# Centring a group norm ahead of a linear recurrence, by a matrix in the turning of the values

## What is computed

```python
def wkv_scan(s0, r, w, k, v, a, b, reverse):
    def step(s, inp):
        r_t, w_t, k_t, v_t, a_t, b_t = inp
        sa = jnp.einsum('bhvk,bhk->bhv', s, a_t)
        s = s * w_t[:, :, None, :] + sa[..., :, None] * b_t[:, :, None, :] + v_t[..., :, None] * k_t[:, :, None, :]
        return s, jnp.einsum('bhvk,bhk->bhv', s, r_t)
...
def rwkv_out(y, r, k_sum, v, xg, g_up, r_k, gn_g, gn_b):
    mu = jnp.mean(y, axis=-1, keepdims=True)
    var = jnp.mean(jnp.square(y - mu), axis=-1, keepdims=True)
    yn = ((y - mu) * lax.rsqrt(var + GN_EPS)).reshape(bsz, t, D_RWKV) * gn_g + gn_b
    bonus = (jnp.sum(r * k_sum * r_k, axis=-1, keepdims=True) * v).reshape(bsz, t, D_RWKV)
    return (yn + bonus) * g
```

## Time and profile before

| what | us |
|---|---|
| three runs | 2332.89, 2322.07, 2326.87 |
| median | 2326.87 |
| span of the profiled execution, first to last instruction | 2324.3 |
| TensorE busy | 2102.2 (90%) |
| VectorE busy | 1575.8 (68%) |
| ScalarE busy | 1245.2 (54%) |
| 40 turnings (L582), each | 0.272 |
| 16 records of the mean products (L1377), together | 7.11 |

### The profile page before, as it was taken

How to read it: one execution, slowest core, us unless ns; L and a number is a source line. 1 busy time by engine, 2 the same in 40 slices (tenths; PEclk the granted TensorE clock), 3 DMA queues, 4 the chain that set the end, 5 groups by cost and what they waited for, 6 DMA issues and landing times. The chain is left out here.

```text
span 2324.3 us, 51473 instructions
## 1 busy us (share of the span) xinstructions
PE 2102.2 (90%) x21654; PEld 1675.4 (72%) x21654; DVE 1575.8 (68%) x2324; ACT 1245.2 (54%) x2324; POOL 659.5 (28%) x465
## 2 busy tenths in 40 slices
PE   5999999599999988891799999999958999999989
PEld 3788888477888853681688888888747778866667
DVE  3666654788889746427599999999766846556531
ACT  4422221476677654433688888888645434357530
POOL 0000020566666610114013323323034455400011
PEclk8999999799999999996899999999979999999999
DMA  8222252333222239426599999999845364230032
GB/s 287 59 68 61 71 130 47 74 72 72 64 64 65 58 110 354 146 100 235 208 354 384 389 397 388 387 395 392 280 132 179 105 221 115 88 131 2 2 110 81
DMA packets 164658, 399.63 MB, mean 172 GB/s; under 512 B 13630, under 2 KB 58060, under 8 KB 164428
## 3 DMA queue, kind: packets, MB, share of 16 engines
q1 hardware_dynamic: 149804, 347.56, 43.0%
q0 software_dynamic: 12224, 44.57, 7.0%
q10 hardware_dynamic: 2400, 4.21, 0.5%
HBM read 348.06 MB, written 46.66 MB: 170 GB/s over the span
## 5 line engine op out<-in xcount | busy, mean ns | idle before, releaser
L1940 DVE TENSOR_TENSOR exp_w_lo<-mixT,exp_w_hi 128x2048 fp32r<-128x2048 f32 x124 | 278.7, 2283 | 23.4 <-ACT exp_w_hi L1897 23.4
L1897 ACT ACTIVATE exp_w_hi<-mixT 128x1024 fp32r<-128x1024 f32 x256 | 255.0, 1053 | 55.8 <-PE banks L1859 38.6
L2153 POOL TENSOR_TENSOR w_lo<-mixT,w_hi 128x512 fp32r<-128x512 f32 (+1 forms) x108 | 145.7, 1370 | 166.6 <-ACT w_hi L2229 163.9
L1859 PE MATMUL banks<-exp_w_hi,xsT_lo 128*128 128x512 f32 x512 | 161.0, 396 | 6.3 <-DVE xsT_lo L1944 6.3
L1859 PE MATMUL banks<-exp_w_lo,xsT_hi 128*128 128x512 f32 x512 | 159.4, 393 | 0.0
L1859 PE MATMUL banks<-exp_w_hi,xsT_hi 128*128 128x512 f32 x512 | 159.3, 393 | 0.0
L1827 POOL DMA_INDIRECT moe_rows<-exp_out,idxT x16 | 25.2, 1573 | 435.7 <-DVE exp_out L1999 435.7
L2211 PE MATMUL banks<-w_hi,h_lo 128*128 128x512 f32 (+1 forms) x320 | 123.5, 386 | 7.8 <-POOL w_lo L2153 5.3
L2211 PE MATMUL banks<-w_lo,h_hi 128*128 128x512 f32 (+1 forms) x320 | 120.3, 376 | 0.0
L2211 PE MATMUL banks<-w_hi,h_hi 128*128 128x512 f32 (+1 forms) x320 | 120.2, 376 | 0.0
L1812 POOL DMA_INDIRECT xs<-xn_rows,idxT x16 | 116.0, 7248 | 14.2 <-DVE idxT L1971 5.6
(11 more groups left out here) (395 smaller groups left out, 5857.7 us busy)
## 6 DMA issues: line engine op xcount, KB each, us to landing
mixT<-in_exp_w_up_dram SPq DMA_DIRECT2D x62, 1024.0 KB, 10.2
mixT<-in_exp_w_gate_dram SPq DMA_DIRECT2D x34, 1024.0 KB, 9.3
mixT<-in_exp_w_down_dram SPq DMA_DIRECT2D x32, 1024.0 KB, 9.2
mixT<-in_w_in_dram SPq DMA_DIRECT2D x96, 256.0 KB, 2.9
ada_w_second<-in_ada_w_dram SPq DMA_DIRECT2D x16, 1024.0 KB, 9.6
kaT<-in_exp_w_down_dram SPq DMA_DIRECT2D x16, 1024.0 KB, 7.1
exp_w<-in_exp_w_down_dram SPq DMA_DIRECT2D x16, 1024.0 KB, 7.4
chunk<-rkv_scratch SPq DMA_DIRECT2D x80, 192.0 KB, 4.0
```

Source lines behind the costliest of these rows:

```text
L1859: mm = pe.matmul(g.ps[bank + q][:, :], lhs[:, kk, :], wide[:, k, q * 512:(q + 1) * 512], start=(kk == 0 and p == 0), stop=(kk == KT - 1 an ...
L1897: last = act.activation(wh[:, n % RH, k, :], w[n % RING][:, k, :], ACT.Copy)
L1940: dve.tensor_tensor(wl[:, n % RH, :, :], w[n % RING], wh[:, n % RH, :, :], ALU.subtract).then_inc(lo_ok, 1)
L2153: pool.tensor_tensor(wl[:, q % SR, 0:width(q)], w[:, q % WR, 0:width(q)], wh[:, q % SR, 0:width(q)], ALU.subtract).then_inc(w_lo, 1)
```

## The change

`phase_project` makes a matrix `centre` = identity - `head`/64 on VectorE, and each block of values is turned by a plain f32 product with `centre` as the moving operand in place of a transpose with the identity. The stored r, k, v (`rkv_scratch`) stay as they were. In `phase_heads_out` the mean products, their subtraction on VectorE, their places in the bank order and ScalarE's wait for them go.

```diff
+        centre = sb(nc, ctx, "centre", [P, P])
...
+        (centred,) = sems(nc, ctx0, "pj_centre")
...
                               sig[:, :].rearrange("p (j k) -> p j k", j=2), ALU.mult).then_inc(cond_ok, 1)
+            dve.scalar_tensor_tensor(centre[:, :], g.c("head"), -1.0 / HD, g.c("ident"), ALU.mult, ALU.add).then_inc(centred, 1)
             dve.wait_ge(cols, 2)
...
             def turn_values(j, i):
                 q = 3 * j + i
                 pe.wait_ge(mixed, FIRST + 1 + j)
+                if q == 0:
+                    pe.wait_ge(centred, 1)
...
-                    mm = pe.transpose(g.ps[6 + q % 2][:, m * P:(m + 1) * P], mix[:, kept_no[8 + j] % MR, b * P:(b + 1) * P], g.c("ident"))
+                    mm = pe.matmul(g.ps[6 + q % 2][:, m * P:(m + 1) * P], mix[:, kept_no[8 + j] % MR, b * P:(b + 1) * P], centre[:, :],
+                                   start=True, stop=True)
...
-    kinds = (["mean"] * NP_ + ["var"] + (["a0", "a1"] * HP + ["gate"] * HP) * 2 + ["wide", "bonus"] * NP_)
+    kinds = (["var"] + (["a0", "a1"] * HP + ["gate"] * HP) * 2 + ["wide", "bonus"] * NP_)
...
-            for i in range(NP_):
-                pe.matmul(into("mean", i)[:, :], g.c("head"), tok(g.yT, i), start=True, stop=True).then_inc(done["mean"], 1)
             pe.wait_ge(picked, HP + 3)
...
             for i in range(NP_):
-                freed(act, "mean", i)
                 act.activation(tok(sq, i), tok(g.yT, i), ACT.Square).then_inc(squared, 1)
...
-            for i in range(NP_):
-                b = bank("mean", i)
-                dve.wait_ge(done["mean"], i + 1)
-                dve.scalar_tensor_tensor(tok(g.yT, i), g.ps[b][:, :], -1.0 / HD, tok(g.yT, i), ALU.mult, ALU.add).then_inc(free[b], 1)
             freed(dve, "var", 0)
```

More of the change, by code:

```diff
@@ L1269, in phase_heads_out @@
         rk_in = ring_sems(nc, ctx0, "ho_rkv_in", 2)
-        done = {k: ctx0.new(f"ho_{k}") for k in ("mean", "var", "a", "gate", "wide", "bonus")}
+        done = {k: ctx0.new(f"ho_{k}") for k in ("var", "a", "gate", "wide", "bonus")}
         free = ring_sems(nc, ctx0, "ho_bank_free", NBANK)
```

## The result

The changed kernel took 2337.11 us (median of 8 runs, 2331.21 to 2339.09) against 2326.97 us for the kernel before (8 runs, 2320.44 to 2332.89): a ratio of 1.004, 95% interval 1.0024 to 1.0056, or 5.6 to 13.0 us slower. The forecast, +4.5 us, lies outside that interval; the time lies inside the range given for it, and within 0.5% of the kernel before. So the question is where another 5 us came from. The changed kernel's profiled execution has a span of 2330.3 us (time 2332.44), at the lower end of its runs.

The account below looks back on a forecast made before the run. TensorE, never idle, bounds the projection; the loads of `ada_w_second` bound the heads' stage. Turning +4.5, matrix 0 and heads 0 on the runs' median 2326.87 gave 2331.4 us (+0.19%), range 2324 to 2341.

Parts of the forecast that it names:

- The turning: Projection on TensorE: 40 transposes (4.3 us) become 80 product records at 0.110 us (8.8 us), +4.5 us.
- The router's rows: Nearest profiled f32 products, each with its own 128x128 weights; they gave 0.110 us per record for the new products.
- Rival C: Projection: a centring product costs more than two records' spacing, total 2339.9 or 2346.6 us; chance 0.05.
- VectorE and the new matrix: Projection: VectorE's 1.1 us longer wait per head is caught up; building the matrix hides behind another wait; cost 0.
- The heads' stage: Variance comes 3.7 us earlier, but DMA waits swallow it; booked 0, bounds 0 and the whole 5.4 us.
- the second block's DMA at 867.59: Heads' stage: `multiply(0)` waits for the second block of `ada_w_second`, so neither it nor the rates move.
- the 1 us that I had named as a sign of being wrong: The forecast is wrong if the heads' stage changes its length by over 1 us.
- One reading behind the booking: Heads' stage: SyncE held 39.69 us by its own queued loads, not TensorE, so loads don't start sooner; booked 0.
- TensorE's clock: Start of heads' stage: 3.9 us of idleness likely halves the clock; variance ends 2.3 us later, still before the DMA; cost 0.
- the 4.5 us I reckoned with: Heads' stage: assumed time at half clock rate, making the sixteen variance records end 2.3 us later, at 865.6.
- Rival B: Heads' stage: clock stays low at its start, +4.5 to +14.7 us with the turning, up to 2341.6 us; chance 0.07.
- The recurrence: Stage behind a barrier after the projection: it merely starts later by what the turning adds; no term of its own.

Follow-up runs that it names:

- heads_only: Changed kernel with the values turned by transposes as before, heads' stage without mean products, so the group norm's mean is left out: 2324.07 us, ratio 1.0004.
- before_pad80: Kernel before with 20 tiny f32 products (80 instructions) ahead of TensorE's first transpose: 2332.36 us, ratio 1.0032.
- before_pad128: Kernel before with 32 tiny products in TensorE's idle times of the first 38 us, a shift by 128 places: 2335.61 us, ratio 1.0041.
- before_pad192: Kernel before with 48 tiny products in TensorE's idle times ahead of the projection, a shift by 192 places: 2327.19 us, ratio 1.0005.
- after_pad176: Changed kernel with 44 tiny products (176 instructions) in TensorE's idle times of the first 38 us, a shift by 256 in all: 2328.5 us, ratio 1.0015.

## Why the prediction was right or wrong

**The turning: right.** 0.112 us a record against 0.110, 80 of them, and +4.9 us for the stage (six profiles with the product, 353.0 to 353.8, mean 353.4; of the kernel before 348.4 and 348.7) against +4.5. From each group's first start to the start of the next tile product, the eight groups hold TensorE for 8.24 us after and 3.73 before, +4.5 us: the forecast's sum to the tenth. The stage's other 0.4 us lie outside the turning and were not followed. The router's rows were the right ones to go by: weights of 128 columns loaded for every record, hidden. Rival C has fallen, and with it the Trainium skill's factor of four for this use: eight blocks hold the engine 1.70 us instead of 0.79, a factor of 2.2.

**VectorE and the new matrix: right.** 1.1 us per head more in VectorE's wait, nowhere passed on to TensorE in the projection.

**The heads' stage: right in the sum, wrong in a step.** With the mean products the stage took 77.5 to 79.5 us (eight profiles, mean 78.4), without them 77.4 to 79.9 (five profiles, mean 78.1). So 7.1 us of TensorE and 5.4 us of VectorE went, and the stage kept its length within its scatter: the loads set it. `heads_only` says the same by the clock on the wall, 1.0004. But I said that the second block's DMA at 867.59 would hold `multiply(0)`, so that the rates would not move. They moved by 2.3 us. The wait of 0.66 us in the row told only that the block was the last to come in that execution, not by how much; the cover that did hold was the next one, the wait at 880.84 in the earlier trace rows. One pair of profiles doesn't show this, since that wait too ended 2.9 us earlier after (885.72), but all of them do: with the mean products the rates begin 14.1 to 15.8 us into the stage (mean 15.5) and this wait ends at 24.3 to 26.3 (mean 24.9); without them the rates begin at 10.9 to 13.5 (mean 12.2) and it ends at 23.4 to 25.7 (mean 24.5). Of 3.4 us, 0.4 are left. Nor was the stage's first -2.1 us a gain, though it is over the 1 us that I had named as a sign of being wrong: a single profile of this stage scatters by as much. One reading behind the booking was mistaken: the 39.69 us of the earlier trace rows are the time over which SyncE issued twelve loads, and in 10 waits, 25.5 us in all, it waited there for TensorE's `multiply`, not for its own queue. It cost nothing that can be seen, with the stage's DMA share at 1.02.

**TensorE's clock: right.** It fell as the engine idled and returned some 6 us after work resumed, longer than the 4.5 us I reckoned with, and cost nothing. Rival B has fallen: the variance still ended earlier than before.

**The recurrence: wrong, and the time was inside the range by luck.** The step that failed is the sentence that the recurrence, "behind a barrier, moves too". I took a later start for the only thing that a stage inherits. It also inherits its place in TensorE's instruction stream, and that was worth +6.1 us (shift 80, mean of five 450.2, against 444.2 for the three at shift 0; the first lie within 1.4 us, the second within 2.5). 4.9 + 6.1 - 0.3 = 10.7 us stands against the measured 10.1. None of my rivals had this term, and the range held the time only because B and C had widened it. The number of instructions that a step issues was in my sum as time on its engine, not as places.

What makes the places matter is shown in three steps. A shift alone reproduces the loss, without any part of the change. A shift by 256 undoes it within the scatter (446.6 and 445.6 us), with every part of the change still in. And the stalls are tied to the fetching of instructions, by two things that the kept traces hold and the views above don't print.

First, a trace holds the start and the duration of each packet of the instruction queue. Before, there are 172, of 16384 bytes each. TensorE's records (weight loads, products, semaphore and drain instructions) are 44032, which is 256.0 for each packet: by this count the packets are TensorE's instructions, in blocks of 256. Second, the stalls stand at one place of these blocks. I numbered TensorE's records from the kernel's start, and took the waits marked "issue" of the weight loads in the recurrence, from 30 us into it on (its first two waits, 4.3 and 3.7 us long, stand ahead of that). Over the thirteen profiles 107 of them last 0.5 us or longer. All 107 stand on a record whose number, divided by 256, leaves 193, 194 or 195, and all end 1.2 to 1.9 us after a packet has landed. (Why 193 and not 0 is not known: the numbering starts at the first record, not at the first instruction.) The longest of some kernels:

| kernel (shift) | line, us into the recurrence | stall, us | number mod 256 | stall's end, us after the packet landed |
|---|---|---|---|---|
| before (0) | L1158, 74.2 | 1.10 | 194 | 1.25 |
| after (80) | L1183, 233.0 | 1.31 | 194 | 1.43 |
| before_pad80 (80) | L1183, 231.7 | 1.61 | 194 | 1.42 |
| before_pad128 (128) | L1185, 315.9 | 1.69 | 194 | 1.80 |
| before_pad192 (192) | L1166, 192.2 | 1.03 | 194 | 1.52 |
| after_pad176 (256) | L1172, 297.7 | 1.14 | 194 | 1.44 |

A shift changes which line of the kernel stands at that place. Where it is a dense group of small products (32 products of 64x64 and their 32 weight loads are issued in 0.69 us), TensorE waits for its next block. The Trainium skill ("Runtime: NRT & Kernel Launch", Instruction fetch mechanics) says that instructions come in blocks of 16 KiB, 256 of them; the traces agree. It also calls the cost of crossing a block mostly hidden. That holds for most crossings here, but not for all: a recurrence has 97 packets, and 12 to 26 of them have a stall over 0.15 us at that place.

How much a stall costs is not shown. The stalls over 0.15 us at that place sum to 5.8 us in the shortest recurrence (440.7) and to 12.7 us in the longest (452.8), but to 10.7 us before and 11.6 us after, 0.9 us for a loss of 4.9. In the stretch from 223 to 310 us all the marked waits of the weight loads are 4.7 us before, 8.9 after and 9.5 in `before_pad80`, about as much as the turns there lengthen; elsewhere stalls went away and the stage didn't gain. My reading is that the cost depends on what waits behind the stalled group; no run here shows it.

## What to carry to other kernels

A stage is not the same stage when instructions are added in front of it: in a long unrolled stream of small products, the places of 256-instruction blocks were worth up to 9 us of 445 here, more than the work that the change added. So judge a small change by the stages that it touches, and test a loss elsewhere with a kernel that has only the padding. Work taken out of a stage that its loads set gives nothing back, so a price paid elsewhere for it, here a transpose turned into a two-pass product, is paid in full. And a short wait for a DMA in one trace is no proof that the DMA would still be late 2 us earlier.

## What the hardware did that I had not expected

- TensorE's instructions came in 172 packets of 16384 bytes, one for 256 records. All 107 stalls of 0.5 us or longer in the recurrences stood at the same place of such a block, 1.2 to 1.9 us behind a packet.
- The recurrence took 440.7 to 452.8 us with the same number of records and TensorE busy for 393.8 to 397.2 us, by how many TensorE instructions stood ahead of it (0, 80, 128, 192 or 256 places).
- 128x128 transposes hold TensorE for 0.099 us each and plain f32 products of the same size for 0.212 us each (two records), weight loads included.
- 7.1 us of TensorE's and 5.4 us of VectorE's work taken from a stage at 1.02 DMA share left its length at 78 us.
